# SSD scan of a hybrid decoder layer: which engine forms the masked decay increments of the prompt tiles

## The reference, cut to what matters

```
dai = dt * a                                   # per token and head
cum = cumsum(dai)
decay[i, j] = exp(cum_i - cum_j)   for i >= j, else 0
m = (C_i . B_j) * decay * dt_j
y = m @ x  +  (C @ h) * exp(cum)               # inside the tile, and from the state
w = exp(last - cum) * dt
h = exp(last) * h + (w * x)^T B
y = (y + D * x) * silu(z), normalised per group
```

## Time and profile before

| | us |
|---|---|
| median of 3 runs | 3423.53 |
| lowest, highest | 3420.49, 3431.26 |
| profiled execution, first to last instruction (span) | 3424.9 |
| TensorE busy in it | 3151.4 |
| VectorE busy | 1114.9 |
| GpSimd busy | 837.9 |
| ScalarE busy | 674.0 |

### The profile page before, as it was taken

One profiled execution on the slowest core, in us unless ns is written; L12 is line 12 of the kernel. 1 busy time (PEld: TensorE's weight loads), 2 busy tenths in 40 slices (PEclk: granted clock), 3 DMA queues, 4 the chain that ended last, 5 costly groups with the idle time before them and its releaser, 6 DMA issues.

```text
span 3424.9 us, 41907 instructions
## 1 busy us (share of the span) xinstructions
PE 3151.4 (92%) x18248; PEld 2883.0 (84%) x18248; DVE 1114.9 (33%) x1792; ACT 674.0 (20%) x1248; POOL 837.9 (24%) x495
## 2 busy tenths in 40 slices
PE   5899999889889999978789998988898999999998
PEld 4788999578578999864379998886698999999998
DVE  5776012322321137328831204112003222322223
ACT  3444001212310012115520112123102000000002
POOL 2222232121021233223312213410022233222330
PEclk9999999798898999987899999999999999999998
DMA  3011221111112323221222422202311111111111
GB/s 93 25 38 38 64 64 55 41 36 51 41 36 74 96 76 83 59 73 44 66 78 83 139 66 74 86 25 94 109 38 32 49 44 44 44 44 50 44 44 59
DMA packets 282376, 205.24 MB, mean 60 GB/s; under 512 B 27851, under 2 KB 259340, under 8 KB 282194
## 3 DMA queue, kind: packets, MB, share of 16 engines
q1 hardware_dynamic: 205664, 112.21, 11.6%
q10 hardware_dynamic: 76530, 90.36, 8.2%
HBM read 167.39 MB, written 35.15 MB: 59 GB/s over the span
## 4 chain that ended last, share of the span: by engine, by line
PE 58%; DVE 6%; ACT 3%; DMA 3%; issue 1%; POOL 0%; ACTq 0%; DVEq 0%; POOLq 0%
PE PS L502 40%; PE PS L1057 8%; DVE WK L1779 1%; PE PM L867 1%; PE PS L895 1%; PE PS L763 1%; PE PS L951 1%; PE PS L1000 1%; PE PS L1016 1%; PE PS L523 1%; PE PM L523 1%; PE PS L787 1%; ACT WK L1670 1%; PE PS L914 1%; DMA Wr<-in_w_xv 1%
## 5 line engine op out<-in xcount | busy, mean ns | idle before, releaser
L502 PE MATMUL PS<-Hh,Wh 128*128 128x384 f32 x3408 | 770.7, 335 | 34.2 <-DVE WK L1779 14.2
L443 POOL CAST Wh<-Wr 128x1024 fp32r<-128x1024 f32 x198 | 233.7, 1180 | 2262.5 <-DMA Wr<-in_w_in 972.7
L502 PE MATMUL PS<-Hh,Wl 128*128 128x384 f32 x3408 | 756.5, 331 | 0.0
L502 PE MATMUL PS<-Hl,Wh 128*128 128x384 f32 x3408 | 751.0, 329 | 0.0
L502 PEld LDWEIGHTS PS<-Hh,Wh 128*128 128x128 f32 x3408 | 586.7, 191 | 44.3 <-issue 29.6
L502 PEld LDWEIGHTS PS<-Hl,Wh 128*128 128x128 f32 x3408 | 587.4, 190 | 0.0
L502 PEld LDWEIGHTS PS<-Hh,Wl 128*128 128x128 f32 x3408 | 583.3, 191 | 0.0
L445 POOL TENSOR_TENSOR Wl<-Wr,Wh 128x1024 fp32r<-128x1024 f32 x214 | 529.1, 2473 | 96.7 <-ACT Wh L1623 80.8
L1779 DVE SCALAR_TENSOR_TENSOR WK<-WK,PS 128x384 f32<-128x384 f32 (+1 forms) x252 | 122.9, 528 | 1091.0 <-PE PS L502 698.3
L2314 DVE TENSOR_TENSOR X<-X,PS 128x384 f32<-128x384 f32 (+1 forms) x288 | 135.9, 528 | 225.8 <-PE PS L1057 123.0
L1090 ACT ACTIVATE WK<-PS 128x384 f32<-128x384 f32 (+1 forms) x96 | 38.5, 474 | 526.7 <-PE PS L502 524.5
(11 more groups left out here) (366 smaller groups left out, 3720.8 us busy)
## 6 DMA issues: line engine op xcount, KB each, us to landing
Wr<-in_w_in SPq DMA_DIRECT2D x84, 512.0 KB, 3.9
merged<-WK ACTq DMA_DIRECT2D x22, 544.0 KB, 4.3
WK<-merged ACTq DMA_DIRECT2D x22, 544.0 KB, 5.5
Wr<-in_w_ffn_gate SPq DMA_DIRECT2D x22, 512.0 KB, 3.8
Wr<-in_w_ffn_up SPq DMA_DIRECT2D x22, 512.0 KB, 3.8
Wr<-in_w_ffn_down SPq DMA_DIRECT2D x22, 512.0 KB, 3.7
WK<-in_cache_mem_k ACTq DMA_DIRECT2D x8, 1024.0 KB, 5.1
WK<-in_cache_mem_v ACTq DMA_DIRECT2D x8, 1024.0 KB, 4.9
```

Of the source, the lines that this page charges most:

```text
L443: pool.tensor_copy(Wh[:, n % SLOTS], Wr[:, n % SLOTS]).then_inc(w_hi, 1)
L502: mm = pe.matmul(pset(name)[:, g, 0:n], L[:, w % SLOTS, k, :], R[:, k, t0:t0 + n], start=(k == 0 and i == 0), stop=(last and k == DT - 1 a ...
```

## The change

GpSimd gets a `decay_steps(q)` of its own, the same 128x1024 product, for q = 0 to 15. It forms steps 0 and 1 ahead of everything else of the scan, once z's first half tile is loaded and dt is done. For q from 2 on it waits for the products of step q-2 (as VectorE did), forms the increments of q and then goes on to `weight_x(q)`. VectorE's `decay_steps` stays for the sample steps 16 and 17 alone, and its calls for the prompt are gone. The waits of TensorE (`r`) and of everyone else are as they were.

```diff
@@ gpsimd
+            def decay_steps(q):
+
+                c, g = divmod(q, 2)
+                pool.tensor_tensor(RM(q), bc(DTK[:, 1, c, 8 * g:8 * g + 8], P), mid(m_le[:], 8), ALU.mult)\
+                    .then_inc(S("r"), 1)
+
+            pool.wait_ge(S("z_in0"), 16)
+            pool.wait_ge(S("dt_done"), 1)
+            decay_steps(0)
+            decay_steps(1)
             weight_x(0)
             weight_x(1)
             for q in range(2, 2 * TT):
+                ready(pool, f"sy{q - 2}")
+                decay_steps(q)
                 weight_x(q)
@@ vector
             def decay_steps(q):
 
-                c, g = divmod(q, 2)
-                n = P if c < TT else TS
-                le = m_le if c < TT else s_le
-                dve.tensor_tensor(RM(q), bc(DTK[0:n, 1, c, 8 * g:8 * g + 8], n), mid(le[:], 8), MUL)\
+                g = q % 2
+                dve.tensor_tensor(RM(q), bc(DTK[0:TS, 1, TT, 8 * g:8 * g + 8], TS), mid(s_le[:], 8), MUL)\
                     .then_inc(S("r"), 1)
@@ vector
-            decay_steps(0)
             tile_sums(0)
-            decay_steps(1)
             matrices(0)
             matrices(1)
             for q in range(2 * TT):
                 ready(dve, f"sy{q}")
-                if q + 2 < 2 * TT:
-                    decay_steps(q + 2)
                 if q:
                     dve.wait_ge(S("y_std"), q)
                 outputs(q)
```

## The result

The changed kernel takes 3468.64 us (median of 4 runs, 3465.57 to 3474.51). The kernel before, run beside it, took 3425.93 us. The ratio is 1.0119, 95% interval 1.0099 to 1.0139: some 41 us slower. The prediction had 3442 us, 18.8 more than before, and a range that ended at 3462. The sign was right and the size was less than half of what came.

What follows compares the result with a forecast made beforehand. TensorE bounds the whole span, but a ring of waits the scan; through GpSimd's queue the loop grows 18.9 us, last increments +0.5, start -0.6: 18.8 more, 3443.7 profiled, median 3442 us, range 3425 to 3462.

Steps and rivals of the forecast that it cites:

- VectorE is the fullest engine of the stretch, and its load is not the path: Prompt scan: VectorE busy 147 of 177 us; taking 24 us of busy time off it changes nothing on the path.
- The increments at 2.55 us: GpSimd's 128x1024 product in each scan step: 2.35 us plus 0.2 for meeting VectorE's outputs; from below 2.08.
- The estimate of 2.25: The same GpSimd product by the Trainium skill's measured 4497 ns for 2048 elements: 2.25 us.
- The lock: GpSimd and VectorE holding each other up when their products overlap: 0.2 us added to GpSimd's increments, ends 0 to 0.9.
- The new ring: GpSimd's queue in the scan: increments, decays, x's load, weighting, next increments; 8.7 us plus decays, 10.7 at full clock.
- the old ring: Scan step through increments, decays, sums in every second step and products: 8.6 or 10.1 us with GpSimd's increments.
- After, with the clock of before: Sum over the scan loop's 13 intervals, two of 16.35 us and seven decays of 1.98: 156.7 us, 18.9 more.
- the case: TensorE's clock falls more often in the scan, seven decays at 1.2 GHz: +12.6 us, 3455 us; chance 0.23.
- Rival 2: Scan at full clock throughout: loop 128 us at low ends, 3413 us, or 3425 us in milder form; chance 0.16.
- Rival 3: GpSimd and VectorE block each other over whole instructions in the scan: 18.5 us more, 3461 us; chance 0.08.
- Rival 4: x's load lands before the increments want GpSimd: about 9.4 us a step, some 10 us less, 3413 us; chance 0.03.
- The start, -0.6: Start of the scan: GpSimd skips VectorE's eight small products but is slower in the first: -0.6 us, between -1 and +1.

Runs made afterwards that it cites:

- three fillers: Changed kernel with three filler matmuls of 128x512, result unread, on TensorE ahead of every wait for the increments; 3423.31 us, 0.9988 of the kernel before.
- transposes late: Changed kernel with GpSimd's increments of q ahead of the weighting of q-1 and TensorE's transposes of y behind the decays, no filler matmuls; 3434.15 us, 1.0026.
- even steps only: Changed kernel with GpSimd forming only the increments of even steps 2 to 14, VectorE those of the odd ones; 3429.63 us, 1.0009 of the kernel before.
- odd steps only: Changed kernel with GpSimd forming only the increments of odd steps 3 to 15, VectorE the even ones and steps 0 and 1; 3471.08 us, 1.0112.

## Why the prediction was right or wrong

- *VectorE is the fullest engine of the stretch, and its load is not the path.* Right. It got 27.9 us less busy in the 120 us of the loop shown (fewer steps fit in, too) and the kernel got slower.
- *The increments at 2.55 us, from below 2.08.* Too high. They took 1.90 us in most steps, under the lower bound that two 128x512 products gave, and 2.34 to 2.35 in two. The estimate of 2.25 beside it was too high as well: 1.90 is 1.6 times VectorE's 1.21 to 1.23, not twice. The lock was looked for on GpSimd's side, +0.2 in every step; it fell there in those two, and on VectorE in the others.
- *The new ring.* Right as a mechanism, at full clock: 10.5 us a step with the increments behind the weighting against 10.7 in the sum (in part by the luck of two errors that cancel), and its parts: load issue to GpSimd's start 1553.39 to 1556.07 = 2.68 (2.7 taken), weighting 3.2 (3.35 taken). But five of 14 increments, not most, stand behind it in the changed kernel; the prediction itself had named increments at the products' end in most steps as a sign that it is wrong. At full clock, with three fillers, 13 of 14 stand behind it, so the reason is the next point: with products at 1.2 GHz the old ring is as long.
- *"After, with the clock of before."* This is the step that failed. The sum kept two intervals of 16 us and seven decays of 1.98. There were five and none. The clock of the stretch, kept at 0.82, came at 0.60 in the 120 us above and 0.62 from 1520 to 1697. 28.5 of the loop's 38.8 us are the clock, and most of the 8.3 us behind it too: with three fillers that part takes 73.0 us and not 79.5. The prediction had written down the gap of 3 to 4.4 us in one place, and the row of the clock's fall, and yet gave the case 0.23 and priced it at the seven decays alone, 3455 us. What it left to a clause, that the products go slow too and each such interval costs 4 to 6 us, was the greater part: three more such intervals at 15.75 instead of 10.7 are 15 us.
- *Rival 2*, a clock that stays up, is what the fillers make by force: 0.9988 on the changed kernel, near the 3425 us given for it. It did not come by itself.
- *Rival 3*, blocking over the whole instruction, is half right: the block is complete, but it falls on the instruction that comes second, and that is VectorE's where GpSimd starts at the products' end. L2137 took 1.67 us instead of some 0.7. The increments at 1574.78 came second, behind an L2137 that ended at 1575.37, and took 2.34 us instead of 1.90. Hence also VectorE's busy time: the prediction took 24 us off it, the trace of before has 27.9 in these 16 products, and it fell by 7.9. Standing counts as busy; the 16 L2137 took 20.7 us together where they had taken 12.4.
- *Rival 4* is out: GpSimd waited for x's load in 14 steps as before, 89 us in all where 98 were before and some 65 forecast.
- *The start, -0.6.* The loop began 0.4 us later. Small either way.

What is open: what makes the clock fall at one gap and not at the next. The length of the one wait ahead of the decays doesn't decide it: on the kernel before, waits of 1.32 us stood ahead of decays of 1.98 us (1601.12) and of 3.78 us, the kernel with transposes late had both behind 2.03 us, and the run with even steps only had full clock behind 2.79 us. What the runs show is a tendency over the whole loop: 0.7 to 1.5 us more in each step took the clock from 0.82 to 0.66, and with waits of 2.5 to 3.6 us in all odd steps (odd steps only) it was 0.66 too.

```profile
1601.12 1.98 PE L763 MATMUL PS<-Ylf,m_gt 128*128 128x512 f32 x4 [1.32 <-DVE Ylf L2099]
```

## What to carry to other kernels

Where TensorE's granted clock already wavers in a stretch, no forecast may keep the clock of before: a change to the gap ahead of its matmuls, whichever engine makes it, can be first a change of the clock, here nearly three times the latency. Before moving work to an idle engine, follow what stands ahead of it in that engine's list and what that waits for; half of this move cost nothing that can be told and the other half cost 1.1%, and they differ in how late the increments come out from behind the weighting. And a run with filler matmuls splits clock from latency to a few us; here it was also worth 0.35% on the kernel before.

## What the runs showed of the hardware

- TensorE's clock fell with gaps far shorter than a step: 120 us of the changed kernel's loop ran at 0.60 with 100.93 us of TensorE busy, and at 0.99 with 112.32 busy when fillers stood in the gaps.
- A GpSimd product of 128x1024 with two broadcast operands took 1.90 us, less than two of its products of 128x512 (2 x 1.04) and less than its 128x1024 subtraction without broadcasts, L445 (2.34 at the least).
- Some of VectorE's instructions stood until GpSimd's product had ended: the scaling of 0.49 us took 2.10, L2137 1.67. It goes the other way too: GpSimd's product took 2.34 us where L2137 had started first. An output that reads PSUM and one small SBUF operand, L2134, took its 0.69 us beside GpSimd (1547.67). The Trainium skill (SBUF — State Buffer, Who interferes with whom) says that the shared port pair is an exclusive lock for a whole instruction, against VectorE's two-port modes and its instructions with two SBUF inputs; the trace agrees on the block and on who stood; in which mode an instruction ran no view here shows.
